# Weight slabs given in parts, the combination of sparse attention moved, gelu by halves, and another order of buffers

## What is computed

```python
def reference(x, ...):
    for l in range(DEPTH):                                   # 2
        proj = rms_norm(x, attn_norm[l]) @ w_in[l]           # 512 x 6804
        o_nsa, o_s5, o_gdn, o_sb = ...                       # each 512 x 256
        for m, o_m in enumerate((o_nsa, o_s5, o_gdn, o_sb)):
            merged = merged + gates[:, :, m] * (o_m @ w_branch[l, m])
        x = x + merged @ w_out[l]
        x = x + swiglu_ffn(rms_norm(x, ffn_norm[l]), w_gate[l], w_up[l], w_down[l])

def nsa_mixer(...):      # per block of 128 queries
    s_s, s_w = q_rot @ k_selected, q_rot @ k_window          # masked softmax of each
    return gb[..., 0:1] * o_c + gb[..., 1:2] * o_s + gb[..., 2:3] * o_w

def s5_mixer(...):
    y = gelu(C_re x_re - C_im x_im + d * u)                  # 512 x 256
    z = y @ glu_w
    return z[..., :256] * sigmoid(z[..., 256:])
```

## The kernel before

| buffer | before | by 64 | after | by 64 |
|---|---|---|---|---|
| hH, hL | 52032, 68416 | 0 | 171680, 188064 | 32 |
| wH, wL | 92992, 105280 | 0 | 204448, 216736 | 32 |
| raw | 84800 | 0 | 106144 | 32 |
| arena | 126624 | 32 | 122528 | 32 |
| pj | 183968 | 32 | 35648 | 0 |

## Time and profile before

### The profile page before, as it was taken

One profiled execution on the slowest core, in us unless ns is written; L12 is line 12 of the kernel. 1 busy time (PEld: TensorE's weight loads), 2 busy tenths in 40 slices (PEclk: granted clock), 3 DMA queues, 4 the chain that ended last, 5 costly groups with the idle time before them and its releaser, 6 DMA issues.

```text
span 2081.9 us, 25541 instructions
## 1 busy us (share of the span) xinstructions
PE 1987.4 (95%) x9988; PEld 1597.1 (77%) x9988; DVE 1118.3 (54%) x1702; ACT 779.1 (37%) x1182; POOL 421.8 (20%) x240
## 2 busy tenths in 40 slices
PE   7998989999999999999999989999999999999999
PEld 5677977567677888888876879766777778888887
DVE  7956557553366555543359365566433755555422
ACT  5442252553254332222254422526432533223221
POOL 3436012232153000000034350122321610000000
PEclk9999999999999999999999999999999999999999
DMA  5332012212163333333343210122121622323333
GB/s 200 116 117 67 9 57 78 76 51 82 50 225 101 99 96 97 96 106 102 109 164 97 85 58 16 61 66 91 52 76 56 237 91 91 101 91 102 102 101 101
DMA packets 60973, 196.45 MB, mean 94 GB/s; under 512 B 10560, under 2 KB 11072, under 8 KB 58688
## 3 DMA queue, kind: packets, MB, share of 16 engines
q1 hardware_dynamic: 44832, 152.49, 23.2%
q10 hardware_dynamic: 16032, 42.41, 5.4%
HBM read 176.01 MB, written 18.87 MB: 94 GB/s over the span
## 4 chain that ended last, share of the span: by engine, by line
PE 82%; DVE 10%; ACT 3%; POOL 2%; issue 1%; DMA 1%; POOLq 0%; SPq 0%; ACTq 0%; DVEq 0%; PEldq 0%
PE bank L489 21%; PE bank L491 21%; PE bank L490 21%; PE bank L728 2%; PE bank L708 2%; PE bank L958 2%; PE bank L846 2%; PE bank L919 1%; PE bank L718 1%; DVE arena L1805 1%; PE bank L827 1%; PE bank L855 1%; DMA raw<-weights 1%; DVE arena L1466 1%; PE bank L836 1%
## 5 line engine op out<-in xcount | busy, mean ns | idle before, releaser
L489 PE MATMUL bank<-hH,wH 128*128 128x512 f32 (+1 forms) x1536 | 616.4, 401 | 21.5 <-DVE hL L1432 9.6
L491 PE MATMUL bank<-hH,wL 128*128 128x512 f32 (+1 forms) x1536 | 603.4, 393 | 0.0
L490 PE MATMUL bank<-hL,wH 128*128 128x512 f32 (+1 forms) x1536 | 603.3, 393 | 0.0
L2035 POOL TENSOR_TENSOR wL<-raw,wH 128x1024 fp32r<-128x1024 f32 (+1 forms) x114 | 274.4, 2411 | 1182.9 <-ACT wH L1061 1182.8
L1061 ACT ACTIVATE wH<-raw 128x1024 fp32r<-128x1024 f32 (+1 forms) x276 | 288.1, 1046 | 256.0 <-PE bank L491 214.2
L489 PEld LDWEIGHTS bank<-hH,wH 128*128 128x128 f32 (+1 forms) x1536 | 290.7, 189 | 98.7 <-issue 24.2
L491 PEld LDWEIGHTS bank<-hH,wL 128*128 128x128 f32 (+1 forms) x1536 | 289.8, 189 | 64.5 <-issue 0.5
L490 PEld LDWEIGHTS bank<-hL,wH 128*128 128x128 f32 (+1 forms) x1536 | 290.9, 189 | 61.7 <-issue 2.6
L1423 DVE TENSOR_TENSOR wL<-raw,wH 128x1024 fp32r<-128x1024 f32 x162 | 213.5, 1318 | 213.0 <-ACT wH L1061 212.3
L491 PE MATMUL bank<-hidH,wL 128*128 128x512 f32 x352 | 140.4, 399 | 0.0
L1064 ACT ACTIVATE gst<-bank 128x512 f32<-128x512 f32 x64 | 38.2, 597 | 269.5 <-PE bank L491 269.5
(11 more groups left out here) (398 smaller groups left out, 2811.1 us busy)
## 6 DMA issues: line engine op xcount, KB each, us to landing
raw<-weights SPq DMA_DIRECT2D x279, 512.0 KB, 3.5
gates<-gst ACTq DMA_DIRECT2D x64, 256.0 KB, 2.4
gload<-gates ACTq DMA_DIRECT2D x16, 1024.0 KB, 7.1
arena<-weights ACTq DMA_DIRECT2D x10, 512.0 KB, 5.3
xT<-x SPq DMA_DIRECT2D x4, 512.0 KB, 5.8
pj<-weights ACTq DMA_DIRECT2D x4, 512.0 KB, 3.9
out<-xT SPq DMA_DIRECT2D x8, 256.0 KB, 4.3
const<-constants SPq DMA_DIRECT2D x1, 1100.5 KB, 7.3
```

The lines of the kernel that those rows point to most:

```text
L489: mm(out, a[0], b[0], start=start, stop=False)
L490: mm(out, a[0], b[1], start=False, stop=False)
L491: return mm(out, a[1], b[0], start=False, stop=stop)
L2035: tt_(l, x, h.bitcast(F32), SU).then_inc(slab_taken[i % RING], 1)
```

## The change

Six edits. (1) On TensorE `part(n)` issues n of the eight row groups of a slab, so that a slab can lie on both sides of a wait: behind the last chunk of the delta rule 6 groups, the sum of squares, then 2; in NSA 2 groups inside and 2 behind the first scores, 4 ahead of each `nsa_output` and 4 behind it. (2) ScalarE copies the S5 input in the first two chunks, two quarters in each, instead of one quarter in each of four. (3) Gelu of S5 goes half by half on ScalarE and VectorE. (4) VectorE's `combine` of blocks 0 to 2 comes behind the next two maxima. (5) The last `combine` comes behind six low parts of the merge, and the last `nsa_output` behind three of the four products of the first merge tile. (6) The buffers lie in another order.

```diff
@@ buffers
         const, pack, vt
+        pj = sb("pj", [P, NPJ, S])
+        sbv = sb("sbv", [P, NT, 256])
+        gst = sb("gst", [P, 2, S])
         xT = sb("xT", [P, KT, S])
-        hH, hL, gload, raw, wH, wL
...
+        raw = sb("raw", [P, RING, KT, P])
         comp = sb("comp", [P, 4, S])
-        pj, sbv, gst
+        arena = sb("arena", [P, 12288])
+        hH, hL, gload, wH, wL
@@ TensorE
+                    def part(n):
+                        for _ in range(n):
+                            if not open_tile:
+                                open_tile.extend((0, slab(FILLERS[filled[0]]), stream_bank()))
+                            k, w, b = open_tile
+                            last = mm3(b[:, :], parts(w, ALLP, k), parts(h2p, ALLP, k), k == 0, k == KT - 1)
+                            open_tile[0] += 1
...
+                    part(6)
                     for i in range(2):
                         pe.wait_ge(*of("head_sq", 1 + i + 1))
                         mm(PS[2 + i][:, :], blk, o_sq[:, i, :], start=True, stop=True).then_inc(q["head_ss"], 1)
-                    fill(FILL["oss"])
+                    part(2)
...
-                    nsa_scores(0, range(H))
+                    nsa_scores(0, (0, 1))
+                    part(2)
+                    nsa_scores(0, (2, 3))
+                    part(2)
...
                             if qt:
+                                part(4)
                                 nsa_output(qt - 1)
...
-                        fill(FILL["nsa"][m])
+                        part(8 if br else 4)
...
-                    nsa_output(NT - 1)
...
+                            if x == 3:
+                                nsa_output(NT - 1)
@@ ScalarE
-                        for t in range(4):
-                            last = act(uc[32 * t:32 * t + 32, 2 * tt:2 * tt + 2, :], u_in[32 * tt:32 * tt + 32, :, :, t], ACT.Copy)
-                        last.then_inc(q["u_chunks"], 1)
+                        for x in (2 * tt, 2 * tt + 1) if tt < 2 else ():
+                            for t in range(4):
+                                last = act(uc[32 * t:32 * t + 32, 2 * x:2 * x + 2, :], u_in[32 * x:32 * x + 32, :, :, t], ACT.Copy)
+                            last.then_inc(q["u_chunks"], 1)
...
+                    fill(FILL["s5"][0])
+                    gelu_square(0)
+                    fill(FILL["s5"][1] - 1)
+                    gelu_tanh(0)
+                    fill(1)
+                    gelu_square(1)
+                    gelu_tanh(1)
@@ VectorE
-                        if m and m % 2 == 0:
-                            combine(qt - 1)
                         if m + 1 < 2 * NT:
                             nsa_maxima(m + 1, (2, 3))
+                        if m and m % 2 == 0:
+                            combine(qt - 1)
...
-                    combine(NT - 1)
                     for j, (m, k) in enumerate(OUT_AT):
+                        if j == 6:
+                            combine(NT - 1)
                         v.wait_ge(*of("o_high", j + 1))
```

More of the change, by code:

```diff
@@ L234, in program @@
         powers = sb("powers", [P, 128])
-        arena = sb("arena", [P, 12288])
+        raw = sb("raw", [P, RING, KT, P])
         comp = sb("comp", [P, 4, S])
         bt = sb("bt", [P, 8, 2, P], at="comp")
-        pj = sb("pj", [P, NPJ, S])
-        sbv = sb("sbv", [P, NT, 256])
-        gst = sb("gst", [P, 2, S])
+        arena = sb("arena", [P, 12288])
+        hH = sb("hH", [P, KT, S], F32R)
+        hL = sb("hL", [P, KT, S], F32R)
+        gload = sb("gload", [P, 4, 4, S], at="hH")
+        wH = sb("wH", [P, SPLIT, KT, P], F32R)
+        wL = sb("wL", [P, SPLIT, KT, P], F32R)
         oH = sb("oH", [P, 8, S], F32R, at="arena")
@@ L533, in _ @@
                     filled = [0]
+                    open_tile = []
+                    def part(n):
[5 more added lines that the diff above has]
+                            open_tile[0] += 1
+                            if k == KT - 1:
+                                last.then_inc(q["slab_done"], 1)
+                                open_tile.clear()
+                                filled[0] += 1
                     def fill(n):
                         for _ in range(n):
+                            assert not open_tile
                             name = FILLERS[filled[0]]
@@ L792, in _ @@
                         fill(FILL["chunk"][tt])
+                    assert FILL["oss"] == 1
+                    part(6)
                     for i in range(2):
@@ L946, in _ @@
                             last.then_inc(q["pct_ps"], 1)
-                        fill(FILL["nsa"][m])
+                        assert FILL["nsa"][m] == 1
+                        part(8 if br else 4)
                         if br == 0:
@@ L1261, in _, with gelu_square, gelu_tanh @@
                     act(s5_cos, s5_cos, ACT.Sin, scale=-SIN_SCALE, bias=TWO_PI / 4).then_inc(q["trig_done"], 1)
-                    for g in range(2):
-                        fill(FILL["s5"][g])
-                    for i in range(2):
+                    def gelu_square(i):
                         a.wait_ge(*of("y5_ps", i + 1))
                         act(y5b[:, i, :], PS[6 + i][:, :], ACT.Square).then_inc(q["y5_sq"], 1)
-                    for i in range(2):
+                    def gelu_tanh(i):
                         a.wait_ge(*of("y5_ready", i + 1))
                         act(y5b[:, i, :], y5b[:, i, :], ACT.Tanh, scale=GELU_C).then_inc(q["y5_tanh"], 1)
+                    fill(FILL["s5"][0])
[5 more added lines that the diff above has]
+                    gelu_tanh(1)
                     fill(FILL["glu"])
@@ L1934, in _ @@
                             nc.vector.tensor_copy(npt[:, kb, :], PS[4 + x % 2][:, :]).then_inc(q["pt_ready"], 1)
+                        if m + 1 < 2 * NT:
+                            nsa_maxima(m + 1, (2, 3))
                         if m and m % 2 == 0:
                             combine(qt - 1)
-                        if m + 1 < 2 * NT:
-                            nsa_maxima(m + 1, (2, 3))
                         if m % 2 == 0:
```

## The result

The changed kernel takes 2059.8 us (median, 2056.4 to 2062.3) against 2086.0 us of the kernel before in the same comparison: the ratio is 0.9871, interval 0.9849 to 0.9894. The span of the profiled execution is 2060.0 us, 21.9 less than before's.

What follows compares the result with a forecast made beforehand. TensorE, busy 95% of the span, was taken to bound the kernel. Schedule terms of -26.0 us, layout +27.1 and some -0.5 for better-covered waits gave net +0.6 on 2087.3: 2088 us, range 2074 to 2098.

Steps and rivals of the forecast that it cites:

- G: Order of buffers: moving operands beginning 32 bytes past a multiple of 64 slow TensorE's matmuls, +27.1 us over both layers.
- Rival 2: Moving operand and weights standing alike by 64 bytes is what counts: 7.3 us faster, 2054 us; chance 0.06.
- Rival 1: The layout costs nothing, the two rates come from something other than the buffer's place: 2061 us; chance 0.11.
- A: End of the delta rule: wait for the squares goes, a new one of some 1.7 us comes; -3.8 us a layer.
- B: Gelu by halves: TensorE's wait shrinks to 0.2 us and the half clock goes; -6.8 us a layer.
- C: First scores of NSA: four groups inside the waits remove them and the slow clock; -3.4 us a layer.
- D: Outputs of NSA blocks 0 to 2: four groups ahead of each cover most of the waits; -3.9 us a layer.
- E: End of NSA: later combination delays the gates' fetch and the merge's chain; +4.5 us a layer, bounds +1.9 and +6.
- rival 3: Slower: half clock behind the new wait of A, E's chain at its upper bound; 2095 us, chance 0.20.
- Rival 4: E cheaper, at its lower bound, with C and D whole: 2080 us; chance 0.10.

Runs made afterwards that it cites:

- order_alone: The kernel before with nothing but the changed kernel's order of buffers: 2084.0 us, ratio 1.0006 to the kernel before.
- lift: The kernel before with arena and all buffers behind it 160 bytes further up, so that everything begins alike: 2079.5 us, ratio 0.9958.
- w256: The kernel before with wH, wL and all buffers behind them 256 bytes further up: 2086.0 us, ratio 0.9997.
- w128: The kernel before with wH, wL and all buffers behind them 128 bytes further up: 2106.7 us, ratio 1.0092.
- all64: The kernel before with every buffer's start rounded up to 64 bytes in place of 32: 2085.8 us, ratio 1.0014.
- undo_A: The changed kernel with the end of the delta rule as before, whole slab and quarter copies in each chunk: 2067.1 us, 7.3 over the changed kernel.
- undo_B: The changed kernel with gelu on both halves together again: 2074.0 us, 14.2 over the changed kernel.
- undo_CD: The changed kernel with whole slabs in sparse attention and the combination of blocks 0 to 2 ahead of the maxima again: 2076.5 us, 16.7 over the changed kernel.
- early_end: The changed kernel with edit 5 taken back, last combination ahead of the low parts again: 2048.8 us, ratio 0.9806 to the kernel before.
- w64: The kernel before with wH, wL and all buffers behind them 64 bytes further up: 2110.8 us, ratio 1.0118.
- h32: The kernel before with hH and hL 32 bytes further up: 2106.2 us, ratio 1.0106.
- wL128: The kernel before with wL and all buffers behind it 128 bytes further up, wH still like hH and hL: 2098.5 us, ratio 1.0058.

## Why the prediction was wrong

**The step that failed is G, the order of buffers.** Forecast +27.1 us, measured -1 to +4 (order_alone's interval). The reading was that a moving operand that begins 32 bytes past a multiple of 64 costs 6.67 ns. The two rates of the earlier trace rows and their difference were right, and they do come from the place of buffers. But a comparison of hL with hidL changes two things at once, the moving operand's remainder by 64 and its distance to the weights, and I took the first. The rows could not tell the two apart; the price rested on one pair of rows, and I gave it the whole value and not a chance. lift, w256 and w128 show that the distance by 256 bytes decides. It was 0 for h in both orders.

Rival 2 came nearest in kind, likeness of moving operand and weights, with a chance of 0.06; its 64 bytes were wrong (all64), and its gain of 7.3 us did not come: with hidL unlike a group of hid gets only from 0.700 to 0.697, and most of what oH and oL save is taken back in the waits for mLow (order_alone). Rival 1, 2061 us, is what was measured, though its reason, that the rates do not come from the place, is wrong: the layout costs nothing here because the fast pair stayed fast.

**A, -3.8 us to a layer: right.** 9.0 us were forecast for the stretch and 9.0 came, the new wait of 1.75 us too ("some 1.7"). undo_A gives 3.7.

**B, -6.8: right.** The wait is 0.35 us, forecast 0.2; no half clock; the second half ends at 355.5. The first step of the second half took 2.24 us in place of 0.42, while GpSimd was in a subtraction (346.42 to 348.81), as the forecast had it. undo_B gives 7.1.

**C and D, -3.4 and -3.9: right, a little small.** The first scores' stretch is 9.7 us, as forecast. D left 0.7 us of waiting that did not appear: no wait stands at the outputs of blocks 0 to 2. undo_CD gives 8.4 in place of 7.3.

**E, +4.5: mechanism right, size too small.** The fetch came 4.4 us later, the low part was blocked by GpSimd (six took 5.45 us, forecast 5.6 from 587.4 to 593.0), and the combination ended 6.3 us after the last values, forecast 6.4. But the price was taken only down the chain of the merge. It ends in a wait of 3.76 us on TensorE, and behind that the clock is low: the next 13 matmuls take 5.7 us and not the 3.1 of full clock, so some 2.6 us more in layer 0, and half as much in layer 1. This was in no term and only as "1.5 more" in rival 3. 6.7 and 6.0 us were measured, above the upper bound of 6 in one layer. That the half clock behind the old last output goes away (0.53 from 591.4 to 595.0 before) pays some of it back; in layer 1 after has half clock there too (0.53 behind 1593.7).

**Rival 3**, half clock behind the new wait of A, did not come: granted clock 1.00 behind 1.75 us. It let the clock decide from about 1.5 us of waiting on; the runs show no such length (see the end). Its row for the 2.13 us, 0.44 us for two small matmuls, could not tell either: the last output's row has the same 0.44, and half clock sets in 0.7 us later. The window gives 1.00 behind the 2.13. Rival 4's terms add up to 2 x 2.6 + 2 x (0.3 + 0.7) = 7.2 us and not 8; nothing rests on it. **The sum of the schedule**, -26.0, stands against -26 measured; it is right partly by luck: E's error of 2 us (by the time) to 4 (by the traces) is set off by C and D and the rest.

## What to carry to other kernels

Before a difference in rate is priced as the property of one buffer, list every other thing in which the two rows differ, and give the price a chance. For fp32r matmuls of 512 columns on this chip, let moving operands and weights begin alike by 256 bytes: one line of padding gave 7 to 9 us here. A step that feeds a rigid chain (the gates' fetch, GpSimd's sums) belongs ahead of work that could be hidden elsewhere, and a wait at the end of such a chain has to be priced with and without half clock behind it: it stood behind mLow's wait of 2.07 us in lift and not behind that of 2.07 in early_end.

## What the runs showed of the hardware

**The rate goes by how the two operands lie to each other.** With the moving operand and the weights alike by 256 bytes a matmul takes 0.2267 us; where all three of a group are unlike it takes 0.2333 or close to it (0.2313 to 0.2343 as the mean of a group's three), at the granted clock of 1.00 (lift, w128, w64, h32 and the table). The Trainium skill, "SBUF — State Buffer", section "Who interferes with whom", gives TensorE two independent read ports, one for the moving operand and one for the weights, and says that it waits for no one. In these runs the pace does go by how the two operands lie to each other, by 6.67 ns a matmul; whether it is the ports that meet is not shown. "TensorE: Matmul & The Clock Gate", section "Wait — 56ns, not 53.3ns?", of the Trainium skill gives 215.7 ns from start to start for 512 columns at the upper clock; the fp32r matmuls here, each with its own weights, take 226.7 at best.

**Open:** what a difference costs in between. By the rule of own or loaded weights a group of hid in the changed kernel should take 0.687 and takes 0.697, and w128's h takes 0.698 and not 0.700; m of after takes 0.703. In wL128 m and hid lie to their weights in the same way (224 bytes to wH, 96 to wL), and yet a group of m takes 0.694 and one of hid 0.700; so the starts by 256 are not all that counts. In before's hid, where all three matmuls pay, the distances are 0.231, 0.231 and 0.238. Also, the times pay less than the rates say: h32's rates make 28 us and its profiled execution was 30 us longer than before's (2111.9 against 2081.9), but its median only 22 us (18.6 to 25.7 by the interval); wL128's rates make 1536 x 0.0125 = 19 us and its profiled execution was 24 longer (2105.7), but its median only 13 (9 to 16). So the reading of wL128 rests on the distances of its groups and not on its time.

**The clock.** Waits that were followed by half clock: 1.94 us (0.53 in before, 0.59 in early_end), 3.76 us (0.56), 5.20 us (0.50). Not followed by it: 1.75 us (1.00) and, in before, 2.13 us (1.00). Two waits went both ways: 1.26 us ahead of the first oH matmul, 1.00 in layer 0 of after and 0.53 in layer 1; and 2.07 us for mLow, 1.00 in early_end and 0.57 in lift. So neither the length of the last wait nor the instructions before it decide alone: the 1.26 us stand behind the same work in both layers, and both waits of 2.07 behind an unbroken row of mH matmuls. What else decides is open.
